# First loads of a two-layer diffusion step in another order on two queues, with two tiles normed ahead of the filter's phases

## The reference

```python
mod_lat = (jax.nn.silu(c) @ ada_w[l] + ada_b[l])          # and mod_ctx from c_ctx
shift1, scale1, gate1, shift2, scale2, gate2 = jnp.split(mod, 6, axis=-1)
h = _rmsnorm(x, norm1_g) * (1 + scale1) + shift1
z = h @ w_in                       # 2048 columns: q, k, v, hyena, gMLP
...
# hyena filter, from constants and small weights alone
h = jnp.sin(fr * (feats @ w1 + b1))
h = jnp.sin(fr * (h @ w2 + b2))
h = (h @ w3) * window
```

## Time and profile before

| | us |
|---|---|
| median of 3 runs | 1878.19 |
| lowest, highest | 1876.71, 1883.25 |
| the profiled execution | 1872.3 |
| its span, first to last instruction | 1870.5 |
| PE busy | 1746.0 (93%) |
| DVE busy | 672.5 (36%) |
| ACT busy | 348.3 (19%) |
| DMA, mean rate | 290 GB/s |

### The profile page before, as it was taken

The page is one execution under the profiler, slowest core; times in us unless marked ns, Lnnn a source line. Parts: engine busy times, 40 slices in busy tenths (PEclk is TensorE's granted clock), DMA queues, the critical chain, the costliest instruction groups (busy, mean ns, idle before and its releaser), DMA issues.

```text
span 1870.5 us, 50717 instructions
## 1 busy us (share of the span) xinstructions
PE 1746.0 (93%) x23010; PEld 1171.9 (63%) x23010; DVE 672.5 (36%) x1562; ACT 348.3 (19%) x779; POOL 155.2 (8%) x141
## 2 busy tenths in 40 slices
PE   3999988979999999999979999999999999999996
PEld 1777667856666665656547777676566666656653
DVE  4542776651111111211157357765211121211114
ACT  2410256220000000000043105733000000000002
POOL 0200031100000000000002001210000000000000
PEclk9999999989999999999979999999899999999999
DMA  9559210379999999999953732024999999999995
GB/s 340 202 179 330 82 67 24 113 282 408 396 406 394 402 399 397 401 395 407 360 184 105 255 128 92 2 102 160 393 407 393 400 400 398 400 399 407 398 374 214
DMA packets 91887, 542.20 MB, mean 290 GB/s; under 512 B 7504, under 2 KB 12626, under 8 KB 68644
## 3 DMA queue, kind: packets, MB, share of 16 engines
q1 hardware_dynamic: 81220, 502.54, 68.0%
q0 software_dynamic: 10464, 36.51, 6.8%
HBM read 515.50 MB, written 23.53 MB: 288 GB/s over the span
## 4 chain that ended last, share of the span: by engine, by line
PE 73%; DMA 15%; DVE 7%; issue 2%; ACT 2%; POOL 1%; SPq 0%; DVEq 0%; ACTq 0%; POOLq 0%
PE bank L1184 41%; DMA ring<-in_exp_w 14%; PE bank L834 11%; PE bank L1021 5%; PE bank L710 2%; PE bank L1042 1%; PE bank L980 1%; PE bank L1059 1%; PE bank L1203 1%; PE bank L737 1%; PE bank L965 1%; DMA arena_z<-xn_dram,icur 1%; PE bank L869 1%; PE bank L1092 1%; DVE arena_u L1876 1%
## 5 line engine op out<-in xcount | busy, mean ns | idle before, releaser
L1184 PE MATMUL bank<-ring,arena_u 128*32 128x256 f32 x12288 | 678.9, 381 | 3.2 <-DMA ring<-in_exp_w 1.8
L1184 PEld LDWEIGHTS bank<-ring,arena_u 128*32 128x32 f32 x12288 | 400.1, 110 | 263.9 <-issue 5.1
L1184 PE MATMUL bank<-ring,arena_z 128*32 128x256 f32 x6144 | 339.1, 379 | 15.7 <-DMA ring<-in_exp_w 10.4
L1184 PEld LDWEIGHTS bank<-ring,arena_z 128*32 128x32 f32 x6144 | 204.8, 110 | 145.7 <-issue 9.5
L2138 DVE SCALAR_TENSOR_TENSOR arena_z<-bank,gateT,gate 80x512 f32<-80x512 f32 (+1 forms) x60 | 34.2, 609 | 561.2 <-PE bank L1184 561.2
L1485 ACT ACTIVATE arena_z<-bank 128x512 f32<-128x512 f32 x30 | 17.9, 597 | 625.0 <-PE bank L1184 625.0
L2115 DVE TENSOR_TENSOR arena_z<-arena_z,bank 128x512 f32<-128x512 f32 x64 | 48.5, 837 | 199.1 <-PE bank L1184 199.1
L1021 PE MATMUL bank<-ring_r 128*128 128x512 f32 x320 | 100.8, 396 | 0.3 <-DVE arena_h_r L1865 0.3
L666 POOL DMA_INDIRECT x_res<-arena_z,iscat x30 | 43.2, 1439 | 670.5 <-DVE arena_z L2141 670.5
L1496 ACT ACTIVATE arena_z<-bank 32x256 f32<-32x256 f32 (+1 forms) x90 | 33.9, 377 | 296.5 <-PE bank L1184 295.8
L834 PE MATMUL bank<-ring_r,arena_h_r 128*128 128x512 f32 (+1 forms) x240 | 85.9, 358 | 0.0
(11 more groups left out here) (305 smaller groups left out, 1889.0 us busy)
## 6 DMA issues: line engine op xcount, KB each, us to landing
ring<-in_exp_w SPq DMA_DIRECT2D x180, 2048.0 KB, 23.6
ring<-in_ada_w SPq DMA_DIRECT2D x24, 2048.0 KB, 9.7
ring<-in_exp_w SPq DMA_DIRECT2D x48, 512.0 KB, 17.0
ring<-in_w_in SPq DMA_DIRECT2D x8, 2048.0 KB, 20.1
ring<-in_w_out SPq DMA_DIRECT2D x2, 4096.0 KB, 12.8
x_res<-arena_z POOLq DMA_DIRECT2D x10, 512.0 KB, 3.3
xn_dram<-arena_u POOLq DMA_DIRECT2D x10, 512.0 KB, 2.9
arena_z<-x_res POOLq DMA_DIRECT2D x5, 512.0 KB, 3.6
```

The lines of the kernel that those rows point to most:

```text
L1184: mm = pe.matmul(group_out(out, g, slice(q * 32, q * 32 + 32)), x(c, t), slot[s][:, c, w * QUARTER:(w + 1) * QUARTER], start=(c == 0 and g ...
```

## The change

- SyncE issues c, c_ctx, the identity, then ada units 0, 1, 2, unit 3 in two halves of the contraction (semaphores `ada_in` and `ada_half`), w_in group 0 in two halves (`win_in`, `win_half`), x tiles 2 to 4, `dbias` and the window (a semaphore of their own, `taps_in`), w_in group 1, and the rest as before.
- ACT issues seven loads ahead of its Silu: x tiles 0 and 1, `prms`, `fw1`, `fw2`, `fw3`, `feats`.
- Tiles 0 and 1 are normed ahead of the filter's phases. Tiles 2 to 4 are normed among the h1 of the tiles ahead of them, beside the first projections. Their squares go to another scratch buffer.
- On PE ada unit 0 stands between the filter layers, and both layers behind each other no longer lead; the transposes of tiles 0 and 1 stand ahead of unit 0. The first modulation step waits for phase(1) as well (`f_pre`).
- `row(0)` and `row(1)` wait for each unit apart. DVE's rests of w_in group 0 are split 1 and 3 instead of 2 and 2 (pairs of chunks) around tile 0's h1.

The diff, without the renamed counts of layer 1 (`prm_in` counts 64 a layer instead of 96 there):

```diff
@@ -257,6 +257,9 @@
         cs_done = sem("cs_done")
         cs_zero = sem("cs_zero")
         prm_in = sem("prm_in")
+        taps_in = sem("taps_in")
+        win_half = sem("win_half")
+        ada_half = sem("ada_half")
         fil_in = sem("fil_in")
         mrow_done = sem("mrow_done")
         step_mm = sem("step_mm")
@@ -488,10 +491,14 @@
                 sp.dma_start(fw2, i["hy_f_w2"][l]).then_inc(prm_in, 16)
                 sp.dma_start(fw3, i["hy_f_w3"][l]).then_inc(prm_in, 16)
                 sp.dma_start(feats, i["feats"]).then_inc(prm_in, 16)
-                sp.dma_start(dbias, i["hy_bias"][l:l + 1]).then_inc(prm_in, 16)
+                taps_loads(l)
+
+            def taps_loads(l):
+
+                sp.dma_start(dbias, i["hy_bias"][l:l + 1]).then_inc(taps_in, 16)
                 if l:
                     sp.wait_ge(x_sum, (l - 1) * NT + NT)
-                sp.dma_start(win, i["window"].rearrange("(t p) n -> p t n", p=P)).then_inc(prm_in, 16)
+                sp.dma_start(win, i["window"].rearrange("(t p) n -> p t n", p=P)).then_inc(taps_in, 16)
 
             def late_loads(l):
 
@@ -520,14 +527,18 @@
             sp.dma_start(cvec[:, 0, :], i["c"].rearrange("a (p k) -> (a p) k", k=KC)).then_inc(c_in, 16)
             sp.dma_start(cvec[:, 1, :], i["c_ctx"].rearrange("(p k) -> p k", k=KC)).then_inc(c_in, 16)
             sp.dma_start(cst[:, 0:P], i["consts"][:, 0:P]).then_inc(const_in, 16)
-            sp.dma_start(prms[:, :, :], i["params"].rearrange("l p n -> p l n")).then_inc(const_in, 16)
-            small_loads(0)
-            for t in range(NT):
+            for u in range(3):
+                ada_load(u)
+            last = i["ada_w"][0, :, D + 512:2 * D].rearrange("(p c) n -> p c n", p=P)
+            sp.dma_start(slot[1][:, 0:HALF, 512:1024], last[:, 0:HALF, :]).then_inc(ada_in[1][1], 16)
+            sp.dma_start(slot[1][:, HALF:KC, 512:1024], last[:, HALF:KC, :]).then_inc(ada_half, 16)
+            first = i["w_in"][0, :, 0:512].rearrange("(p c) n -> p c n", p=P)
+            sp.dma_start(slot[0][:, 0:HALF, 0:512], first[:, 0:HALF, :]).then_inc(win_in[0], 16)
+            sp.dma_start(slot[0][:, HALF:KC, 0:512], first[:, HALF:KC, :]).then_inc(win_half, 16)
+            for t in range(2, NT):
                 sp.dma_start(zt[:, t, 0:D], i["x_sample"][0, t * P:(t + 1) * P] if t < 4 else i["x_prompt"][0])\
                     .then_inc(x_in[t], 16)
-            for u in range(4):
-                ada_load(u)
-            w_in_load(0, 0)
+            taps_loads(0)
             w_in_load(0, 1)
             sp.dma_start(cst[:, P:NCST], i["consts"][:, P:NCST]).then_inc(edge_in, 16)
             sp.dma_start(sel[:, :], i["sel"]).then_inc(edge_in, 16)
@@ -707,6 +718,8 @@
                     pe.wait_ge(mod_out, steps_to(k - 1))
                 pe.wait_ge(ada_in[s][h], 16 * sum(REGION[x] == REGION[u] for x in range(u + 1)))
                 for c in range(KC):
+                    if u == 3 and c == HALF:
+                        pe.wait_ge(ada_half, 16)
                     mm = pe.matmul(out[c % 4 * CT:(c % 4 + 1) * CT, :], cs[:, c, :], slot[s][:, c, h * 512:(h + 1) * 512],
                                    start=(c < 4), stop=(c >= 4))
                 mm.then_inc(ada_mm, 1)
@@ -741,7 +754,7 @@
             for l in range(DEPTH):
                 def filter_layer(n):
                     if n == 0:
-                        pe.wait_ge(prm_in, l * 96 + 96)
+                        pe.wait_ge(prm_in, l * 64 + 64)
                     else:
                         pe.wait_ge(f_sin, l * 2 + 1)
                     w, x = (fw1, feats) if n == 0 else (fw2, hid)
@@ -778,14 +791,15 @@
 
                 if l == 0:
                     filter_layer(0)
-                    filter_layer(1)
                     rows_transposed(0)
                     rows_transposed(1)
-                    for u in range(2):
-                        ada_unit(u)
+                    ada_unit(0)
+                    filter_layer(1)
+                    ada_unit(1)
+                    pe.wait_ge(f_pre, 2)
                     mod_step(0)
-                    for u in range(2, 4):
-                        ada_unit(u)
+                    ada_unit(2)
+                    ada_unit(3)
                     mod_step(1)
                 else:
                     rows_transposed(0)
@@ -1231,6 +1245,13 @@
         def _(act):
 
 
+            for t in range(2):
+                act.dma_start(zt[:, t, 0:D], i["x_sample"][0, t * P:(t + 1) * P]).then_inc(x_in[t], 16)
+            act.dma_start(prms[:, :, :], i["params"].rearrange("l p n -> p l n")).then_inc(const_in, 16)
+            act.dma_start(fw1, i["hy_f_w1"][0]).then_inc(prm_in, 16)
+            act.dma_start(fw2, i["hy_f_w2"][0]).then_inc(prm_in, 16)
+            act.dma_start(fw3, i["hy_f_w3"][0]).then_inc(prm_in, 16)
+            act.dma_start(feats, i["feats"]).then_inc(prm_in, 16)
             act.wait_ge(c_in, 32)
             act.wait_ge(cs_zero, 1)
             act.activation(cs[:, :, 0:2].rearrange("p k s -> p s k"), cvec[:, :, :], ACT.Silu).then_inc(cs_done, 1)
@@ -1245,7 +1266,10 @@
 
                 def w_in_rounded(g, a=0, b=KC):
 
-                    act.wait_ge(win_in[g], l * 16 + 16)
+                    if g == 0 and l == 0 and a:
+                        act.wait_ge(win_half, 16)
+                    else:
+                        act.wait_ge(win_in[g], l * 16 + 16)
                     for c in range(a, b, 2):
                         w, high_w = w_group(slot, g, c, l)
                         act.activation(high_w, w, ACT.Copy).then_inc(w_hi, 1)
@@ -1256,7 +1280,7 @@
                         act.wait_ge(x_sum, (l - 1) * NT + t + 1)
                     else:
                         act.wait_ge(x_in[t], 16)
-                    act.activation(squares if l else arena_u[:, 3200:3200 + D], zt[:, t, 0:D], ACT.Square,
+                    act.activation(squares, zt[:, t, 0:D], ACT.Square,
                                    accum_out=ssum[:, t:t + 1]).then_inc(sq1, 1)
                     act.wait_ge(sq1, l * NT + t + 1)
 
@@ -1288,21 +1312,24 @@
                                    ACT.Copy).then_inc(h_hi, 1)
 
                 if l == 0:
+                    square_sum(0)
+                    root(0)
+                    square_sum(1)
+                    root(1)
                     sine(0)
                     sine(1)
-                    act.wait_ge(f_sin, 2)
-                    for t in range(NT):
+                    w_in_rounded(0, 0, 4)
+                    act.wait_ge(mod_out, 2)
+                    h1(0)
+                    h1_rounded(0)
+                    w_in_rounded(0, 4, KC)
+                    for t in range(2, NT):
                         square_sum(t)
                         root(t)
-                    act.wait_ge(ada_mm, 1)
-                    w_in_rounded(0, 0, 4)
-                    act.wait_ge(mod_out, 2)
-                    for t in range(NT):
-                        h1(t)
-                        h1_rounded(t)
-                        if t == 0:
-                            w_in_rounded(0, 4, KC)
-                    act.wait_ge(ada_mm, 2)
+                        h1(t - 1)
+                        h1_rounded(t - 1)
+                    h1(4)
+                    h1_rounded(4)
                 else:
                     act.wait_ge(chunk_used, AHEAD + chunks(l - 1, w3_at(EXPERTS - 1), KC - 1))
                     w_in_rounded(0)
@@ -1544,8 +1571,8 @@
 
             def row(k):
 
-                v.wait_ge(ada_mm, 2 * k + 2)
                 for n in range(2):
+                    v.wait_ge(ada_mm, 2 * k + (n + 1 if k < 2 else 2))
                     ins = v.tensor_copy(mrow[k][:, n * 512:(n + 1) * 512], bank[4 + 2 * (k % 2) + n][:, :])
                 ins.then_inc(mrow_done, 1)
 
@@ -1608,6 +1635,8 @@
 
 
                     v.wait_ge(f3_mm, l * NT + t + 1)
+                    if t == 0:
+                        v.wait_ge(taps_in, l * 32 + 32)
                     src = bank[6 + t % 2]
                     v.tensor_tensor(hfw, src[:, 0:HY], win[:, t, :], ALU.mult)
                     link(v.tensor_tensor(fdif[:, t, :], src[:, HY:2 * HY], win[:, t, :], ALU.mult))
@@ -1664,23 +1693,28 @@
 
                 v.tensor_scalar(nsink[:, :], prm[:, SK:SK + HEADS], -1.0, None, ALU.mult)
                 if l == 0:
-                    v.wait_ge(prm_in, 96)
+                    mean1(0)
+                    normed(0)
+                    mean1(1)
+                    normed(1)
                     phase(0)
                     phase(1)
-                    for t in range(NT):
-                        mean1(t)
-                        normed(t)
                     row(0)
                     mod_taken(0)
                     row(1)
                     mod_taken(1)
-                    w_in_rest(0, 0, 4)
+                    w_in_rest(0, 0, 2)
                     v.wait_ge(mod_out, 2)
-                    for t in range(NT):
```

(14 more changed lines are left out.)

2 lines of the change are left out of this document (1 added, 1 removed).

## The result

The changed kernel takes 1868.81 us (median of 20 runs, 1865.26 to 1877.60) against 1880.53 for the kernel before on the same chips (20 runs, 1871.14 to 1885.46). The ratio is 0.9944, 95% interval 0.993 to 0.9958: 10.5 us faster, with 7.9 to 13.2 in the interval (the two medians alone are 11.7 apart). The forecast was 1868.0 and a gain of 10.4.

The account below looks back on a forecast made before the run. PE, busy 93% of the span, bounds the kernel, so only its waits before projection group 1 count. 13.1 + 0.65 + 1.2 - 3.0 - 1.5 = 10.4 us off the 1878.2 median: 1867.8, say 1868; range 1862 to 1876.

Parts of the forecast that it names:

- Start of the modulation: First modulation transpose on PE: starts at 26.2 instead of 39.35 us, as three norms and a wait leave the path; 13.1 gained.
- Row halves and one rest less: Modulation to first projection: row(1) copies its first half beside unit 3, 0.65 us; one w_in subtraction fewer before h1, 1.2.
- feats late: Filter layer 0, PE's first instruction: feats on ACT's queue lands late beside SyncE's big loads; 1.5 us lost, bounds 0 to 7.
- Rival 1: Small loads share badly: feats lands at 15 to 17.5 us, gain only 3.5 to 7 (1871 to 1875 us); chance 0.15.
- The weights: Loads before the first projection: unit 3 lands at 28.7 us, w_in's first half at 31.4; hidden with 3 us to spare.
- Norm of tile 2: Between first and second projection: its root and table load delay tile 1's h1; 3.0 us lost, bounds 0 and 6.
- wait of about 3 us for tile 1's rests: Sign ahead of the second projection: PE waits about 3 us there, and not at tiles 2 and 3.
- The clock in the units: Modulation units on PE: a pair takes the slower 4.66 us; bounds 1.0 us gained, 2.6 lost (7.28 at 1.2 GHz).
- 2 (the gain given back at every tile): Behind the first projection DVE falls behind at every tile: gain 1 to 4, 1874 to 1877 us; chance 0.11 including 4.
- 3 (ACT's queue starves): ACT's loads wait for SyncE's, feats after 28 us: 6 to 10 us slower, 1884 to 1888; 0.06 with other losses.
- 4 (bytes bound the path anyway): Total load bytes bound the path, so the first modulation step starts as soon as before; chance 0.11 together with 2.
- The prediction's last test: At the end: the forecast is wrong if the gain at w_in group 1 is there and the span does not show it.

Follow-up runs that it names:

- loads-only kernel: Changed kernel's loads with the compute order of the kernel before; median 1885.35 us, ratio to the kernel before 1.0027.
- norm 2 early: Changed kernel with x tile 2 loaded ahead of unit 3's weights and tile 2 normed before row(1); 1867.21 us, ratio to the kernel before 0.9921.
- fillers only: Changed kernel plus eight useless matmuls before the first modulation step and ten instead of six dummies ahead of the projections; 1867.43 us, ratio to before 0.9927.
- phases first: Changed kernel with small loads first on ACT's queue, both phases ahead of the norms of tiles 0 and 1, tile 2 normed early; 1868.22 us.
- three filler kernels: Changed kernel with eight useless matmuls before the first modulation step (1868.99 us); fillers only; and fillers only with norm 2 early added (1864.71 us).

## Why the prediction was right, step by step

That the gain of 10.4 met 10.5 to 0.1 us is luck: the interval is 7.9 to 13.2, and the marks lie 0.4 to 1.5 us to either side of the sum. Against the kernel before, with the feats term taken in, the sum has a gain of 12.25 at the w_in rests (11.33 in the first profiled execution, 13.25 in the second), 13.45 at the first projection (12.47 and 14.39) and 10.45 at the second (10.03 and 11.94).

**Start of the modulation (13.1, less 1.5 for feats: 11.6 predicted).** It gave 11.85 and 12.94. The parts: ACT's issues ended at 4.70 (4.4 predicted), Silu at 6.31 (6.0), tile 1 was scaled at 12.96 (12.8), and phase(0) then waited 1.11 us for PE. From there to L736 it was 13.43 and 12.25 us, 13.4 predicted; the second execution had the shorter unit 0. L736 itself took 1.94 and 1.13 (1.76 before).

**Row halves and one rest less (0.65 and 1.2).** From the end of the units to the second modulation step PE was idle for 1.42 us before and 0.82 now: 0.60. From w_in_rest to the first projection it was 6.25 before and 5.11 now: 1.14. The loads-only kernel, which keeps two rests there, has 6.25 again (55.06 to 61.31).

**feats late (1.5).** It landed at 11.53, between the bounds 8 and 12. phase(0) began 1.1 to 1.2 us after DVE was free. Filter layer 1 came at 20.45 in the first execution, 1.2 us after its sine was done, behind unit 0, and at 19.36 in the second, at once; it took 1.29 us instead of 2.39. Right in place, slightly too dear. The round robin rule of the Trainium skill (DMA: Bandwidth & Descriptors, Queues, rings and completion order) gave an estimate near 8 and no loss. The trace has 11.53; it shows sharing, but not at that price: from 6 us until then ACT's queue moved 0.25 of 1.80 MB, 269 of 1028 packets, and not half. Rival 1 was this mechanism with more weight; it did not come.

**The weights.** By the prediction's own terms unit 3's load lands at 28.1 and not 28.7, and w_in's first half at 30.8; that half came at about 32.9 and 34.6. In the first execution ACT had rounded it 2.6 us ahead of DVE's first rest; in the second there was nothing to spare.

**Norm of tile 2 (3.0).** The second projection began 9.04 us (first execution) and 9.05 (second) after the first, 9 to 10 predicted and 6.60 before: 2.4 lost. Here the size was right and the working only half. ACT's timeline has the predicted pieces: the table load, held 2.13 us for the reciprocal, then h1 of tile 1.

```profile
46.35 1.28 ACT L1290 ACT_TABLE_LOAD   x1 [2.13 <-DVE srec L1656]
...
47.76 1.49 ACT L1296 ACTIVATE arena_h<-bank,mod 128x128 f32<-128x128 f32 x4
```

But PE did not wait 3 us, nor 1.3 at the transposes. PE's timeline:

```profile
49.88 1.04 PE L789 MATMUL bank<-cst,arena_z 128*128 128x128 f32 x8
51.76 0.47 PE L848 MATMUL bank<-ring_r,arena_u_r 128*128 128x512 f32 x1 [0.84 <-DVE arena_h_r L1690]
```

The first projection took 7.16 us instead of 5.73, at a granted clock of 0.83, and arrived at the transposes when they were ready. The norm and the clock cost about the same and lie beside each other. Take away only the norm (norm 2 early: 25.66) or only the clock's loss (fillers only: 27.23), and nothing is won; take away both and 1.8 us come back (phases first: 23.83), 2.6 with the first projection itself delayed (23.07). That the two hide each other rests on one trace of each kernel and on the distance alone; the times do not tell these kernels apart. The prediction had held the clock's effect to the two modulation units; that it reaches the projection was missing, and the wait of about 3 us for tile 1's rests, which it named as a sign, was 0.84. Tiles 3 and 4 were hidden, as said: 5.73, 0.88 and 5.48 us without a gap.

**The clock in the units.** The slower value was assumed (4.66); it was 5.59 and 5.29. The bound of 7.28 held.

**The rivals.** 2 (the gain given back at every tile) fell: one tile loses. 3 (ACT's queue starves) fell: 7.43 us to landing. 4 (bytes bound the path anyway) fell by L736 at 27.50, but has a true core: the weights of w_in bound the path in the changed kernel's second execution (by 0.19 us), and those of unit 3 in two of the three filler kernels (2.12 and 2.71 us).

**Does the head reach the end?** Yes: 9.8 and 11.7 us at POOL's mark in the two traces, 10.5 in the time over 20 runs of each kernel. Over all kernels the gain at POOL's mark lies within the interval of the time, but for the loads-only kernel, 0.1 us outside. The prediction's last test, "and the span does not show it", would by the profiled execution have called the forecast wrong; it was the wrong test, since one execution carries its own granted clock.

## What to carry to other kernels

Move the loads and the work that needs them together: each half alone was worth nothing or less. What was last on the second queue landed late here, so put there in front what is needed first, and check whether one queue with the same order does as well. When removing a wait brings nothing, look for a second one beside it before calling the theory wrong; and compare marks along the way before comparing the ends of two executions.
